# Asking for the mixer's next rows at the first load position, and squaring them ahead of the folding copies

## What is computed

```python
h = rms_norm(x, mix_pre_norm[l])
z = h @ w_in[l]
zp, za, zg, zb, zc, zx = jnp.split(z, split_at, axis=-1)
ya = pool_mixer(zp, pool_maps[l], pool_scale[l])
yb = conformer_conv(za, zg, conf_dw_w[l], conf_dw_b[l], conf_ln_g[l], conf_ln_b[l])
yc = short_gated_conv(zb, zc, zx, sconv_w[l])
y = jnp.concatenate([ya, yb, yc], axis=-1) @ w_out[l]
x = x + rms_norm(y, mix_post_norm[l])
h = rms_norm(x, xattn_pre_norm[l])
y = cross_attention(h, mem_n, xattn_wq[l], xattn_wk[l], xattn_wv[l], xattn_wo[l])
x = x + rms_norm(y, xattn_post_norm[l])
h = rms_norm(x, ffn_pre_norm[l])
y = conv_ffn(h, ffn_w_up[l], ffn_conv_w[l], ffn_w_down[l])
x = x + rms_norm(y, ffn_post_norm[l])
```

## Time and profile before

| | us |
|---|---|
| median of 3 runs | 2801.68 (2799.71 to 2804.89) |
| the profiled execution, its own time | 2806.28 |
| span of the profile, first to last instruction | 2804.5 |
| PE busy | 2591.9 (92%) |
| DVE busy | 1563.3 (56%) |
| ACT busy | 970.7 (35%) |
| POOL busy | 963.0 (34%) |
| mean granted TensorE clock | 0.964 |

### The profile page before, as it was taken

How to read it: one execution, slowest core, us unless ns; L and a number is a source line. 1 busy time by engine, 2 the same in 40 slices (tenths; PEclk the granted TensorE clock), 3 DMA queues, 4 the chain that set the end, 5 groups by cost and what they waited for, 6 DMA issues and landing times.

```text
span 2804.5 us, 33388 instructions
## 1 busy us (share of the span) xinstructions
PE 2591.9 (92%) x11713; PEld 2142.7 (76%) x11713; DVE 1563.3 (56%) x2446; ACT 970.7 (35%) x1565; POOL 963.0 (34%) x394
## 2 busy tenths in 40 slices
PE   6799979979978999989999999999998999999997
PEld 5677767868767777777778887788877888788886
DVE  4987958747726435455624636616366155463362
ACT  5233312222134444443433333333333334233332
POOL 4551200100013333423443443444434434345442
PEclk9999999989989999999999999999999999999999
DMA  7586674565645335244433235333252333253231
GB/s 249 156 306 255 215 261 166 203 240 186 235 179 180 98 141 179 82 157 141 130 98 91 91 99 173 102 90 98 92 184 82 107 91 98 77 168 109 84 100 65
DMA packets 318417, 410.59 MB, mean 146 GB/s; under 512 B 12584, under 2 KB 235069, under 8 KB 305469
## 3 DMA queue, kind: packets, MB, share of 16 engines
q1 hardware_dynamic: 309709, 396.62, 42.4%
q10 hardware_dynamic: 8560, 12.06, 1.3%
HBM read 343.62 MB, written 65.01 MB: 146 GB/s over the span
## 4 chain that ended last, share of the span: by engine, by line
PE 68%; DVE 13%; issue 9%; ACT 5%; DMA 4%; SPq 0%; ACTq 0%; DVEq 0%
PE colb L1369 11%; PE colb L1370 11%; PE colb L1371 11%; PE accb L1369 11%; PE accb L1370 11%; PE accb L1371 11%; PE colb L1403 2%; DVE arena L1113 2%; ACT pair L631 2%; DMA xh<-in_x 1%; DVE arena L1315 1%; ACT junk L646 1%; DVE small L982 1%; DVE xh L990 1%; DVE xh L1051 1%
## 5 line engine op out<-in xcount | busy, mean ns | idle before, releaser
L600 POOL TENSOR_TENSOR pair<-raw,pair 128x1024 fp32r<-128x1024 f32 x387 | 962.1, 2500 | 1810.8 <-ACT pair L631 1810.8
L1369 PE MATMUL colb<-hT,pair 128*128 128x512 f32 x1952 | 771.8, 395 | 41.0 <-issue 37.7
L1370 PE MATMUL colb<-hT,pair 128*128 128x512 f32 x1952 | 767.8, 393 | 0.0
L1371 PE MATMUL colb<-hT,pair 128*128 128x512 f32 x1952 | 767.4, 393 | 0.0
L631 ACT ACTIVATE pair<-raw 128x1024 fp32r<-128x1024 f32 x387 | 405.6, 1053 | 553.6 <-PE accb L1371 403.6
L1369 PE MATMUL accb<-pair,act 128*128 128x512 f32 x1248 | 496.6, 398 | 5.8 <-DVE act L1076 3.5
L1370 PE MATMUL accb<-pair,act 128*128 128x512 f32 x1248 | 491.2, 394 | 0.0
L1371 PE MATMUL accb<-pair,act 128*128 128x512 f32 x1248 | 490.9, 393 | 0.0
L1312 DVE TENSOR_SCALAR arena<-arena,par 128x512 f32<-128x512 f32 x176 | 238.9, 1397 | 442.9 <-ACT arena L914 442.3
L1369 PEld LDWEIGHTS colb<-hT,pair 128*128 128x128 f32 x1952 | 371.6, 190 | 128.0 <-issue 51.4
L1371 PEld LDWEIGHTS colb<-hT,pair 128*128 128x128 f32 x1952 | 370.9, 190 | 78.3
(11 more groups left out here) (132 smaller groups left out, 2042.7 us busy)
## 6 DMA issues: line engine op xcount, KB each, us to landing
raw<-in_ffn_w_up SPq DMA_DIRECT2D x176, 512.0 KB, 3.8
pair<-kept SPq DMA_DIRECT2D x75, 1024.0 KB, 4.9
raw<-in_ffn_w_down SPq DMA_DIRECT2D x176, 256.0 KB, 2.9
kept<-pair SPq DMA_DIRECT2D x25, 1024.0 KB, 6.5
raw<-att_a SPq DMA_DIRECT2D x64, 256.0 KB, 3.1
raw<-att_b SPq DMA_DIRECT2D x64, 256.0 KB, 3.4
raw<-in_w_in SPq DMA_DIRECT2D x17, 512.0 KB, 7.3
xh<-in_x SPq DMA_DIRECT2D x4, 2048.0 KB, 15.9
```

What stands on the lines that cost most here:

```text
L600: nc.gpsimd.tensor_tensor(pair[:, b, 1, :], raw[:, r, :], pair[:, b, 0, :].bitcast(F32), ALU.subtract).then_inc(lo_done, 1)
L1369: nc.tensor.matmul(dst, sh, mh, start=first, stop=False)
L1370: nc.tensor.matmul(dst, sh, ml, start=False, stop=False)
L1371: return nc.tensor.matmul(dst, sl, mh, start=False, stop=last)
```

## The change

In SP's `body` the block that stores the previous result, loads the gain and asks for the next rows moves from load position 5 to position 0 in the mixer (it was at 0 already elsewhere), and with it the reload of `xt` from position 7 to position 2. In ACT's `mix` the four squares of the next rows are taken before the folding copies of `b_rows(0)` and `b_rows(1)`, where they were taken after them.

```diff
             def body(p, t):
                 last = isinstance(t, int)
-                rows_at = 5 if p in MIXES else 0
                 for i in range(SLOTS[p]):
...
                     load(p, t, i + LOAD_AHEAD, last)
-                    if i == rows_at:
+                    if i == 0:
...
-                    if i == rows_at + 2:
+                    if i == 2:
                         sp.wait_ge(x_stored, step_tile.at(p, t, 1) * 16)
                         sp.dma_start(xt[:, :, :], rows(source[p], tile_of(p, t))).then_inc(xt_in, 16)
...
                 round_y(1)
+                next_squares(p, t)
                 b_rows(0)
                 b_rows(1)
-                next_squares(p, t)
                 rest(10)
```

## The result

| | before | after |
|---|---|---|
| median of 3 runs, us | 2801.68 (2799.71 to 2804.89) | 2757.80 (2756.45 to 2759.07) |
| the profiled execution's own time, us | 2806.28 | 2757.80 |
| span, us | 2804.5 | 2756.0 |
| mean granted TensorE clock | 0.964 | 0.975 |

The ratio is 0.9835, with an interval of 0.981 to 0.986. The kernel became faster, as forecast, but by 43.9 us and not by 63.8, and the time lies above the range's end of 2755. A third of the gain is missing.

What follows compares the result with a forecast made beforehand. TensorE, busy 92% of the span, bounds the kernel; its mixer waits for scaled rows can be won. 60.3 us (tiles 1 to 3) + 3.5 (tile 0) = 63.8, so 2801.68 becomes 2737.9; range 2731 to 2746, to 2755 with most of rival 1.

Steps and rivals of the forecast that it cites:

- The rows asked for earlier, squares ahead of the copies, DVE at once: Mixer tiles 1 to 3: rows requested 29 us earlier, squares start without a wait, scaled rows ready 6.6 us before TensorE asks.
- the sum had 60.3: Mixer tiles 1 to 3: total us won from the vanished wait for scaled rows and the slow start of out(0,1).
- The reload of xt, costed at nothing: Mixer tiles 1 to 3: reload at position 2 delays o1, hidden by 2 us; cost zero, other end 4 us per tile.
- My sum: Transfers up to o1's end, from 361.3 in tile 1: 9.96 MB at 398 GB/s, 25 us, o1 landed at about 386.5.
- the forecast's terms: Gains claimed for mixer tiles 1, 2 and 3: 19.7, 20.9 and 19.7 us.
- rival 1: Mixer tiles 1 to 3: o1 late, new TensorE wait of 3 to 5 us each, tile 0 nothing; about 2753 us; chance 0.12.
- Tile 0, +3.5: First mixer tile: 3.5 us won by squares ahead of the copies, between the ends -4 and +6.
- Rival 5: More than forecast: full DMA stretch after 390 goes, with small losses in later waits; about 2728 us; chance 0.06.
- Rival 2: Mixer: rows still land late, or DVE is late; landing 12 us late loses half the gain, about 2770 us; chance 0.06.
- Rival 3: Mixer: late rows make early squares block the folding copies and out(0,0); 4 to 5 us lost per tile, about 2815; chance 0.02.
- Rival 4: SP's queue: position 0 reached no earlier than position 5, so nothing changes; about 2802 us; chance 0.02.

Runs made afterwards that it cites:

- the before's repeat: The kernel before the change, unaltered, run and profiled once more in a third job: 2808.3 us, ratio 1.0003 to itself.

## Why the prediction failed, step by step

**The rows asked for earlier, squares ahead of the copies, DVE at once: right.** SP issued the rows at 365.99 in tile 1, on a clock that runs 2.7 us later than the before's (q1 at 342.81 and 340.08), which is 28 us earlier than 391.67; I had said 29. The squares found the rows there. Both waits of the earlier trace rows are gone from tiles 1 to 3, and the slow start of out(0,1) with them. With the reload out of the way the three tiles gave 61.1 us where the sum had 60.3 (58.3 against the before's repeat).

**The reload of xt, costed at nothing: wrong, and the main cause.** The prediction named the danger and worked it out: o1 landed at 386.5, ready at 390.1, wanted at 392.3, a margin of 2 us. On the changed kernel's clock that is ready at 392.8, wanted at 395.0. It was ready at 397.95: 5.1 us later than the sum said. Two terms of the sum were off.

Stretches of the changed kernel (from:to, length, busy time of PE, PEld, DVE, ACT, POOL, clock, DMA share, GB/s):

```profile
364.30:371.00 6.70, 6.70 (x37) 5.74 (x36) 3.32 (x7) 1.12 (x2) 0.00 (x0) 1.00 0.84 243
371.00:388.70 17.70, 17.70 (x79) 14.62 (x78) 15.36 (x46) 0.66 (x1) 0.00 (x0) 1.00 1.03 412
```

Two more numbers read on this trace: over 364.00 to 394.40 us the DMA engines moved 365 GB/s, over its last 5.7 us 382.

The first 6.7 us of the burst moved 243 GB/s, and only then 412. My sum had 398 from the first moment. And by the time that o1 had landed (364.00 to 394.40 us) the DMA engines had moved 11.09 MB, not the 9.96 of the sum: the other 1.13 are of the loads behind o1, r10's slot and the next, which SP asked for at 387.13 and 392.57 while o1 was still on its way. That is by elimination: nothing else was asked for in that time, and nothing was under way at its start. At 398 GB/s 9.96 MB are 25.0 us; the 1.13 MB more are 2.8, the slow start less the faster rest another 2.5, together 30.3, and 30.4 passed. That accounts for the error of 5.1 us. Nor did ACT catch up before the squares, as the prediction had it: they began at 396.95, where its 389.7 is 392.4 on this clock. That cost nothing, since out(0,0) came later too and the transposes at 413.27 did not wait. The rest of the step held: the reload left at 377.58, which on this clock is inside the 371 to 375 of the prediction, and the store took 12.8 us as in the earlier trace rows.

The price: in tile 1 a wait of 2.79 us and 1.6 us of slow matmuls behind it, 4.4 in all, which is 19.7 - 15.3. Over the three tiles the traces lack 10.4 us against the forecast's terms (13.2 with the before's repeat), and against the kernels that reload behind o1 the changed one takes 10.5 to 11.6 us more in them. That is rival 1, priced at 3 to 5 us per tile (12 in all) and given a chance of 0.12. Its time of 2753 was near the 2754.1 to 2757.8 measured. What failed was to take 2 us for a cover when each of two estimates behind it was off by more than 2 us. A margin smaller than the error of its terms is no cover. The chance of rival 1 should have stood near a half, and the range should have gone past it.

**Tile 0, +3.5: wrong by its half.** It gave 0.1. Its two parts were measured apart: squares early alone give +3.7 (135.25 to 131.53), and rows, gain and reload early take back 3.6. The direction of both had been named. PE's timeline of the changed kernel in tile 0:

```profile
226.00 0.47 PE L1368 MATMUL colb<-hT,pair 128*128 128x512 f32 x1 [1.62 <-POOL pair L599]
...
238.55 1.53 PE L1402 MATMUL colb<-ident,xh 128*128 128x128 f32 x12 [0.97 <-DVE xh L989]
...
242.04 0.66 PE L1402 MATMUL colb<-ident,xh 128*128 128x128 f32 x4 [1.96 <-DVE arena L1176]
```

The first is a wait on a weight's low part, as feared. In the kernel with the squares alone neither it nor the second is there; the third is, with 1.97 us. The loads of r9 now stand behind gain and rows: one goes out at 190.04 where the before had it at 186.30, but 2.9 us of that are the later start of this trace. What is new is how long it takes: its transfer of 15.31 us stands in the chain of work, and ACT rounds it at 205.37, where the before rounded it at 195.21.

**The rest.** The start up to the first kvd matmul was 2.9 us longer in the after profile, which the repeats show to be chance. Attention and FFN kept their length within 1.3 us, as the prediction asked. Rival 5's small further gains are not seen.

**The other rivals.** Rival 2 (rows late) did not come, and with the rows at position 4 it is seen what it costs: 37 us against position 3. Rival 3's mechanism was run with the squares alone and gives a gain of 11.9 us, not a loss; my reason, that the matmuls of out(0,0) then stand behind the wait, was right, but I had not set against it that DVE's scaling runs beside them. Rival 4 falls with the issue at 365.99.

What stays open: why the burst's first 6.7 us move so little. In them SP asks for a slot, the store, the gain and the rows, and the DMA engines are busy for 0.84 of the time, so most of the loss is slow bytes and not idle engines. With the reload late the first 6.5 us show 244 GB/s too, so the reload is not the cause. Whether the store, a write, is was not tried.

## What to carry to other kernels

A transfer that waits for something and is not urgent belongs behind the last urgent load of its queue; ahead of it, it holds that load back: here the reload one position later, behind o1's request, gave some 10 us (58.8 won against 48 on average), and weights first, then the rows, 17 (65.3; its trace shows tiles 1 to 3 as short as there, and a tile 0 shorter by 3.9 to 5.5 us than in the changed kernel's three). When a prefetch is moved forward, ask what is urgent and now stands behind it, and move it only as far as its own slack needs: position 3 was early enough and position 0 too early. And where a step is costed at nothing with a margin, compare the margin with the error of the numbers that make it.

## What was unexpected of the hardware

**The clock after the same short wait.** In two executions of the kernel before, TensorE waits 1.81 us at the same instruction (start of out(1,0)) and goes on. The stretches behind it, first in the profile that the prediction used and then in the repeat (clock is the third number from the end):

```profile
295.53:298.53 3.00, 3.00 (x13) 2.49 (x14) 3.00 (x3) 2.82 (x8) 2.31 (x1) 1.00 0.00 0
```

```profile
298.39:301.39 3.00, 3.00 (x10) 2.41 (x11) 3.00 (x3) 2.82 (x8) 2.30 (x1) 0.71 0.00 0
301.39:304.39 3.00, 3.00 (x11) 2.40 (x10) 3.00 (x5) 1.27 (x4) 0.00 (x0) 0.72 0.00 0
```

The same gap cost nothing in clock in the one. In the other the granted clock was 0.71 and 0.72 over two stretches of 3 us, and within them the matmuls from 300.01 to 303.00 follow each other every 0.43 us, the half rate, and those around them every 0.23. I did not find what decides it. The 19th matmul from the wait on starts 4.20 us after the first of them in the one (299.73) and 5.80 us in the other (304.19): 1.6 us lost. So a short wait can cost more than its own length, and a single trace doesn't tell whether it does.

**A POOL instruction of 2.8 us that took 13.7.** In the repeat the next low part on POOL, 128 x 1024, runs beside DVE's convolution taps:

```profile
306.99 13.68 POOL L600 TENSOR_TENSOR pair<-raw,pair 128x1024 fp32r<-128x1024 f32 x1 [6.30 <-ACT pair L631]
```

In the first profile the same step took 2.76 us at 302.51, also beside DVE's taps (L1113), and TensorE had no wait on it; in the repeat TensorE waits 4.20 us for it, until 320.81. A later wait on ACT's arena (L767) shrinks from 4.72 to 1.14 us in return, and with what the clock loses and gives back behind these waits the stretch is 3.4 us longer.

The two findings go together. In all five traces where the clock stays at 1.00 behind the 1.81 us wait, the POOL instruction takes 2.8 us; in all eight where it falls to 0.63 to 0.71 for the next 3 us, POOL's takes 13.7. The link can be read in the two traces of the before: ACT's rounding waits for the matmuls (1.47 us in the first, 3.10 in the repeat), so POOL starts 6.98 us behind the wait's end in the first and 8.60 in the repeat, and there it ends at 320.67, 2.2 us after DVE's run of taps does (318.47). Whether the later start is what does it, and why, was not tested.

**More than the named limit of the memory.** Over 17.7 us the DMA engines moved 412 GB/s (the stretch above). The Trainium skill (DMA: Bandwidth & Descriptors, Where 436 GB/s comes from) puts transfers to and from HBM at about 358 GB/s, which it works out as half of what a memory stack shared by two cores gives; beside it the section names a measured 425 for a transfer of 16 MB. The measurement decides: for this kernel, which runs on one core, 358 is too low, and 412 lies under the 425 that the prediction did not use. What mattered more was the low rate at the start of the burst, 243.
